# RWKV's state steps: the state is added by an identity product on TensorE, and VectorE only multiplies by the decay

## The chip, the cores and the metric

The kernel runs on one core of one Trainium2 chip. The metric is the device time of one launch in microseconds (us), the median over several runs. A trace of one profiled execution stands beside it. A core has five engines that run their own instruction queues in order and meet at semaphores: TensorE (matrix products; PE in the profile, PEld for its weight loads), VectorE (DVE), ScalarE (ACT), GpSimd (POOL) and SyncE (SP, which here issues transfers).

## The reference, cut to what matters

The program is two transformer-like blocks over 256 tokens of width 1024. The second has an RWKV-7 branch of 8 heads of width 64, whose core is a recurrence over the tokens:

```
def step(S, inp):
    r_t, w_t, k_t, v_t, kk_t, b_t = inp
    sa = jnp.einsum('bhvk,bhk->bhv', S, -kk_t)
    S = S * w_t[:, :, None, :] + sa[..., None] * b_t[:, :, None, :] + v_t[..., None] * k_t[:, :, None, :]
    return S, jnp.einsum('bhvk,bhk->bhv', S, r_t)
```

S is a 64 by 64 matrix for each head. The kernel computes it in four chunks of 64 tokens. Inside a chunk everything is brought into matrix form ahead of time, and only the state goes from chunk to chunk. With keys and values scaled by the decay up to their token, a chunk's end state is (S + btok^T sa + ktok^T vtok) times the decay over the chunk, where sa = xat S + U0.

## The kernel before, in words

The whole program is one `build` function with one hand-ordered instruction list for each engine. There is no planner: what stands ahead in an engine's list is done first, and `wait_ge` on a semaphore holds the engine's whole list. Weights come by SyncE's transfers into a ring of three pages; VectorE and ScalarE split each page into a high and a low part, and TensorE multiplies by them, for most of the span. The small stretch that this change touches is the loop over the four chunks (n = 0 to 3) in the middle of the span, lines 1022 to 1046 on TensorE and 2231 to 2244 on VectorE.

TensorE's list for chunk n: it waits for the state n (`s_sb`); 8 sa products (one for each head, `xat` times `states[n]`, into PSUM banks 2 and 3); it waits until VectorE has added U0 to them and stored sa (`sa_sb`); then 16 state products, for each head `btok` times `sa` and `ktok` times `vtok`, summed in PSUM bank 4 or 5. In chunk 1 the products `y_states(0)` and half of `y_part(0)` (the outputs of the first two chunks) follow, in chunk 2 the other half of `y_part(0)`. Chunk 3 ends after sa, and `y_states(1)` and `y_part(1)` follow.

VectorE's list for chunk n: it waits for the sa products (`sa_mm`) and adds U0 (line 2236); then, for n below 3, it waits for the state products (`ds_mm`), adds `states[n]` to what stands in PSUM into `states[n + 1]` (line 2241), and multiplies that by the decay `wend` in place (line 2242). Ahead of the loop VectorE has `lo_part(2, so, ym_r, ...)`, two instructions of line 1740 that belong to another branch and wait for ScalarE's `ym_hi` (line 1579). Ahead of the loop ScalarE brings U0 from PSUM banks 4 and 5 into SBUF, two instructions of line 1576 that count `u0_sb`. Behind the loop VectorE has four instructions of line 2246, four of 2249 and two of 2256; TensorE's next product (`head_norm`) waits for the last.

All these products are of fp32 numbers. A product of 64 rows deep and 64 wide is a tile of 64*64 in the array, and its place follows from the partitions of its operands (`r0` or `r` for rows) and of its output (`r` or `r0` for columns). In the profile a product is two matmul records and two weight load records. All products are recorded at line 458, the `mm` helper, or at 897 for the transposes.

Of the kernel before, what the change touches and what calls it, by code (L numbers as in the profile page):

```python
# [14 lines left out]
P = 128  # L15
# [11 lines left out]
ALU = mybir.AluOpType  # L27
# [82 lines left out]
def build(nc, t, out):  # L110
    with ExitStack() as ctx:
        S = {n: ctx.enter_context(nc.semaphore(n)) for n in dict.fromkeys(SEMS)}
# [24 lines left out]
        ps = ctx.enter_context(nc.psum_tensor("ps", [P, 8, 512], F32))  # L137

        def at(off, n, base=arena, **kw):
            v = base[:, off:off + n]  # L140
            return v.rearrange(kw.pop("r"), **kw) if kw else v
# [4 lines left out]
        ident = pc[:, 0:128]  # L146
# [12 lines left out]
        def w3(off, a, b=L):  # L159
            return arena[:, off:off + a * b].rearrange("p (a b) -> p a b", a=a)  # L160
# [73 lines left out]
        btok = w3(25120, 2, 512)  # L234
        ktok = w3(26144, 2, 512)
        vtok = w3(27168, 2, 512)
        gram = at(2048, 4096).rearrange("p (n a s) -> p n a s", n=16, a=4)
        mt = at(10752, 1024).rearrange("p (n s) -> p n s", n=16)
        sa = w3(12800, 2, 512)
        yT = w3(13824, 4)  # L240
        states = at(23072, 1280).rearrange("p (n j v) -> p n j v", n=5, j=4)
# [20 lines left out]
        s_sb = at(8192, 4096).rearrange("p (t g n) -> p t g n", t=2, g=16)  # L262
# [39 lines left out]
        wend = small[:, 192:208].rearrange("p (j c) -> p j c", j=4)  # L302
# [140 lines left out]
        def _(pe):  # L443
# [13 lines left out]
            def mm(*args, **kw):  # L457
                mm_last[0] = nc.tensor.matmul(*args, **kw)  # L458
                return mm_last[0]
# [179 lines left out]
            for g in range(3):  # L639
                for q in range(2):  # L640
                    p = ((1, 3), (4, 5), (6, 7))[g][q]
                    pe.wait_ge(loaded[p % RING], 16 * (p // RING + 1))
                    for k in range(4):
                        m = mm(ps[0:2, 4 + g, :], csil[:, 4 * q + k, :], ring[:, p % RING, k // 2, 4 * (k % 2):4 * (k % 2) + 4, :],
                               start=q == 0 and k == 0, stop=q == 1 and k == 3)
                    m.then_inc(S["mod_used"], 1)
                if g == 1:
                    pe.wait_ge(S["pconst_in"], 16)
                    pe.wait_ge(S["start_sb"], START["sum1"])
                    for j in range(4):  # L650
                        for c in range(2):
                            mm(ps[:, 2, 24 + 2 * j + c:25 + 2 * j + c], mcol[c][:, j * P:(j + 1) * P], ones[:, 0:1],
                               start=True, stop=True)
# [30 lines left out]
            for d, kw in enumerate((kw_f, kw_b)):  # L684
                for j in range(4):
                    for tt in range(2):
                        for hh in (2 * j, 2 * j + 1):
                            r = (hh % 2) * 64
                            m = mm(ps[r:r + 64, 2 + d, j * P:(j + 1) * P], kw[:, tt, hh * 64:(hh + 1) * 64],
                                   vc_tok[:, tt, hh * P:(hh + 1) * P], start=tt == 0, stop=tt == 1, skip_group_check=True)  # L690
                m.then_inc(S["state_mm"], 1)
            pe.wait_ge(S["const1_in"], 16)
            for q in range(4):
                mm(ps[:, 4 + q, :], c1("perm"), qraw[:, 2 * q:2 * q + 2, :], start=True,
                   stop=True).then_inc(S["perm_mm"], 1)
# [50 lines left out]
            for n in range(8):  # L746
                b = (2, 3, 4, 5)[n // 2]
                if n % 2 == 0 and b == 5:
                    pe.wait_ge(S["probs"], 8)
                m = mm(ps[:, b, (n % 2) * L:(n % 2 + 1) * L], fT[:, n // 2, (n % 2) * P:(n % 2 + 1) * P], c1("dft_d"),  # L750
                       start=True, stop=True)
# [5 lines left out]
            for gi in range(4):  # L757
                n = 0
                for lt in range(2):
                    for c in range(2):  # L760
                        m = mm(ps[:, 6 + gi // 2, (gi % 2) * L:(gi % 2 + 1) * L],
                               four_a[:, 2 * gi + lt, c * P:(c + 1) * P], dft_l[:, c, lt, :], start=n == 0, stop=n == 3)
# [8 lines left out]
            for q in range(4):  # L771
                pe.wait_ge(S["hn_sq"], q + 1)
                mm(ps[:, (6, 7, 2, 3)[q], :], ones, sq_o[:, 2 * q:2 * q + 2, :], start=True,
                   stop=True).then_inc(S["hn_sqmm"], 1)
# [10 lines left out]
            for k in range(8):  # L785
                if k % 2 == 0:
                    pe.wait_ge(S["xs_sq"], 4 + (k // 2 + 1))
                m = mm(ps[:, 3, 0:L], norm_w[:, k, :], sq[:, k, :], start=k == 0, stop=k == 7)
            m.then_inc(S["xs_mm"], 1)
            for k in range(8):  # L790
                m = mm(ps[:, 2, 0:L], ones, sq[:, k, :], start=k == 0, stop=k == 7)
# [3 lines left out]
            for u in range(6):  # L795
                fm_page(PAGE["rkv"] + u, TURN["rkv"] + u, h)
                if u == 2:
                    pe.wait_ge(S["lora_tanh"], 2)
                    for q in (0, 1, 4, 5):
                        for e in range(2):  # L800
                            m_ = (2 * q + e) % 4
                            half = slice(e * L, (e + 1) * L)
                            if q < 2:
                                m = mm(ps[:, 2 + q, half], wa_up[0:64, m_ * P:(m_ + 1) * P], lora_in[0:64, 0, :], start=True,
                                       stop=True)
                                if e == 1:
                                    m.then_inc(S["lora_mm"], 1)
                                m = mm(ps[:, 4 + q, half], wa_up[64:128, m_ * P:(m_ + 1) * P], zs[64:128, 12, :], start=True,
                                       stop=True)
                            else:  # L810
                                m = mm(ps[:, 2 + q, half], g_up[:, m_ * P:(m_ + 1) * P], lora_in[:, 1, :], start=True,
                                       stop=True)
# [4 lines left out]
            for k in range(8):  # L817
                _, m = three(ps[0:36, T % 2, 0:L], (w_if[0][:, k, :], w_if[1][:, k, :]), (h[0][:, k, :], h[1][:, k, :]),
                             k == 0, k == 7)
# [10 lines left out]
            for tt in range(2):  # L830
                m = nc.tensor.transpose(ps[:, 2, 4 * tt:4 * tt + 4], m_rows[0:4, 4, tt * P:(tt + 1) * P], ident[0:4, 0:4])
            m.then_inc(S["uc_mm"], 1)
            for n in range(4):
                mm(ps[:, 4 + n, :], c2("sel")[0:4, n * P:(n + 1) * P], m_rows[0:4, 5:7, :], start=True,
                   stop=True).then_inc(S["bc_mm"], 1)
# [66 lines left out]
            for m_ in range(8):  # L902
                i, j = m_ // 4, m_ % 4
                for e, par in quarters:
                    r, t0 = blocks[par], i * P + 64 * e
                    m = mm(ps[blocks[e], 6 + par, m_ * 64:(m_ + 1) * 64], ar[r, j, i, 0, blocks[e]],
                           beta[r, j, t0:t0 + 64], start=True, stop=True)
# [30 lines left out]
            for q in range(2):  # L938
                for k in range(8):
                    m = turned(6 + q, k, 8 * q + k)  # L940
# [37 lines left out]
            for i in range(2):  # L978
                for j in range(4):
                    for e, par in quarters:  # L980
                        n = 8 * i + 2 * j + par
                        c = slice((2 * j + par) * 64, (2 * j + par + 1) * 64)
                        m = mm(ps[blocks[par], 2 + 2 * i + e, j * 64:(j + 1) * 64], atok[blocks[e], i, c], XT[blocks[e], n, :],
                               start=True, stop=True)
                m.then_inc(S["xa_mm"], 1)
            for i in range(2):
                for hh in range(8):
                    c = slice(hh * 64, (hh + 1) * 64)
                    for s in blocks:
                        m = mm(ps[s, 6 + i, c], gram[s, 8 * i + hh, 2, :], vtok[s, i, c], start=True, stop=True)  # L990
                m.then_inc(S["xa_mm"], 1)
            pe.wait_ge(S["xa_sb"], 2)
            for i in range(2):
                pe.wait_ge(S["lv_sb"], i + 1)
                for hh in range(8):
                    c = slice(hh * 64, (hh + 1) * 64)
                    for s in blocks:
                        m = mm(ps[s, 4 + i, c], XT[s, 8 * i + hh, :], lv[s, i, c], start=True, stop=True)
# [23 lines left out]
            for n in range(4):  # L1022
                i, r0 = n // 2, (n % 2) * 64
                pe.wait_ge(S["s_sb"], n + 1)
                for hh in range(8):
                    r, j = (hh % 2) * 64, hh // 2
                    c = 256 * (n % 2) + 64 * j
                    m = mm(ps[r0:r0 + 64, 2 + hh % 2, c:c + 64], xat[r:r + 64, j, i, r0:r0 + 64],
                           states[r:r + 64, n, j, :], start=True, stop=True)
                m.then_inc(S["sa_mm"], 1)  # L1030
                pe.wait_ge(S["sa_sb"], n + 1)
                if n == 3:
                    break
                for hh in range(8):
                    r, j, c = (hh % 2) * 64, hh // 2, slice(hh * 64, (hh + 1) * 64)
                    o = ps[r:r + 64, 4 + n % 2, j * 64:(j + 1) * 64]
                    mm(o, btok[r0:r0 + 64, i, c], sa[r0:r0 + 64, i, c], start=True, stop=False)
                    m = mm(o, ktok[r0:r0 + 64, i, c], vtok[r0:r0 + 64, i, c], start=False, stop=True)
                m.then_inc(S["ds_mm"], 1)
                if n == 1:  # L1040
                    turn(TURN["pm"])
                    turn(TURN["pm"] + 1)
                    y_states(0)
                    y_part(0, (0, 1))
                if n == 2:
                    y_part(0, (2, 3)).then_inc(S["y_mm"], 1)
# [25 lines left out]
            for n in range(8):  # L1072
                T = TURN["wq"] + n
                turn(T)
                for s in range(2):
                    m = whole(PAGE["wq"] + n, s, ps[:, T % 2, s * L:(s + 1) * L], ("hraw", 32) if n + s == 0 else None)
# [5 lines left out]
            for n in range(4):  # L1082
                for k in range(4):
                    m = mm(ps[:, 2 + n, k * P:(k + 1) * P], xres[:, 4 * (n % 2) + k, (n // 2) * P:(n // 2 + 1) * P], ident,
                           start=k == 0, stop=False, skip_group_check=True)
# [10 lines left out]
            for tt in range(2):  # L1096
                pe.wait_ge(S["selt_ready"], tt + 1)
                pe.wait_ge(S["placed"], 8)
                for c in range(3):
                    m = nc.tensor.transpose(ps[:, 6 + tt, c * P:(c + 1) * P], selv[:, tt, c, :], ident)  # L1100
# [33 lines left out]
            for q in range(L // 4):  # L1134
                scatter(q)
                n, k = (q - 3) // 14, (q - 3) % 14
# [557 lines left out]
        def _(dve):  # L1694
            V = nc.vector
            TT, STT, TS = V.tensor_tensor, V.scalar_tensor_tensor, V.tensor_scalar
            steps = [0]

            def dv(ins):

                steps[0] += 1
                ins.then_inc(S["dch"], 1)
                dve.wait_ge(S["dch"], steps[0])
# [81 lines left out]
            for q in range(2):  # L1785
                p = 2 * q
# [290 lines left out]
            r = m_rows[0:4]  # L2077
# [153 lines left out]
            for n in range(4):  # L2231
                i, c = n // 2, n % 2
                rr = slice(64 * c, 64 * c + 64)
                dve.wait_ge(S["sa_mm"], n + 1)
                by_row = "p (j e v) -> p e j v"
                TT(sa[rr, i, :].rearrange(by_row, e=2, v=64),  # L2236
                   ps[rr, 2:4, 256 * c:256 * c + 256].rearrange("p e (j v) -> p e j v", v=64),
                   U0[rr, i, :].rearrange(by_row, e=2, v=64), ALU.add).then_inc(S["sa_sb"], 1)
                if n < 3:
                    dve.wait_ge(S["ds_mm"], n + 1)  # L2240
                    dv(TT(states[:, n + 1], states[:, n], ps[:, 4 + c, 0:256].rearrange("p (j v) -> p j v", j=4), ALU.add))
                    TT(states[:, n + 1], states[:, n + 1], wend[:, :, n:n + 1].to_broadcast([P, 4, 64]),
                       ALU.mult).then_inc(S["s_sb"], 1)
                    dve.wait_ge(S["s_sb"], n + 2)
            for m in range(4):
                ins = STT(bon[:, m, :], bon[:, m, :], col("gn_b", m), gT[:, m, :], ALU.add, ALU.mult)
# [405 lines left out]
```

## Time and profile before

| what | value |
|---|---|
| median of three runs | 1713.86 us (1713.19 to 1717.4) |
| the profiled execution's own time | 1715.07 us |
| span in its trace | 1713.2 us |
| mean granted TensorE clock over the span | 0.988 |
| TensorE matmul busy | 1643.1 us, 96% |
| VectorE busy | 1173.3 us, 68% |
| ScalarE busy | 802.0 us, 47% |

Times in the trace run from the start of the span. Busy shares are averages over all stages. The granted clock is a share of the full 2.4 GHz: 1.00 is full, 0.50 is 1.2 GHz. Matmuls are pipelined: a record's duration is its latency, and several records overlap. A tile is written rows*columns of the array, "128*64 128x128" being a tile of 128 rows and 64 columns through which 128 columns of the other operand stream from 128 partitions. "x16" is a count of records.

### The profile page before, as it was taken

To read this page: it belongs to the slowest core of one execution; us is meant where nothing else is said; L and a number is where in the kernel's file an instruction comes from. 1 tells how busy PE (TensorE), PEld (TensorE's weight loads), DVE (VectorE), ACT (ScalarE), POOL (GpSimd) and SP (SyncE) were. 2 spreads that over 40 slices of the span, in tenths; PEclk is the share of its full clock that TensorE was granted. 3 is DMA by queue.
4 is the path that set the end of the run, shared out by engine and by line. 5 is a ranking of instruction groups with operands and counts; after the bars stand their busy time and mean duration, and the time that the engine had idled before them with its cause. 6 is when DMAs were issued, how large, how long until landed. Compare 5 with 4: busy or idle time off the path is not lost.

```text
span 1713.2 us, 32554 instructions
## 1 busy us (share of the span) xinstructions
PE 1643.1 (96%) x12574; PEld 1505.7 (88%) x12574; DVE 1173.3 (68%) x2142; ACT 802.0 (47%) x1221; POOL 99.0 (6%) x124
## 2 busy tenths in 40 slices
PE   7999999999999999979999989999999999999997
PEld 2899978999999999878898877999999999999996
DVE  5646556777756769647498998666666666666665
ACT  2423436566644675324213993444444444444443
POOL 0000000022200001210052000000000000000000
PEclk9999899999999999999999999999999999999999
DMA  8765413545544443203333015555555555555553
GB/s 335 301 240 221 144 53 142 194 172 175 194 173 148 150 146 123 100 4 140 128 127 123 25 50 180 189 193 177 193 186 181 196 178 189 191 178 194 183 184 111
DMA packets 38538, 278.94 MB, mean 163 GB/s; under 512 B 4400, under 2 KB 4528, under 8 KB 5040
## 3 DMA queue, kind: packets, MB, share of 16 engines
q1 hardware_dynamic: 35136, 254.82, 41.5%
q0 software_dynamic: 2304, 16.78, 2.5%
q10 hardware_dynamic: 1008, 6.05, 1.0%
q8 instruction: 68, 1.11, 0.3%
q14 instruction: 22, 0.18, 0.0%
HBM read 276.58 MB, written 1.05 MB: 162 GB/s over the span
## 4 chain that ended last, share of the span: by engine, by line
PE 85%; DVE 8%; ACT 4%; issue 2%; DMA 1%; DVEq 0%; POOL 0%; ACTq 0%; POOLq 0%
PE ps L458 85%; DVE piece L1709 2%; ACT piece L1201 1%; DMA ring<-in_stream 1%; DVE pconst_sb L2453 1%; DVE cols L2453 1%; DVE late L2453 0%; DVE arena L1759 0%; DMA small<-in_cT 0%; ACT arena L1240 0%; DVEq L2453 0%; DVE arena L1795 0%; ACT L1236 0%; DVE arena L1776 0%; DVE arena L1828 0%
## 5 line engine op out<-in xcount | busy, mean ns | idle before, releaser
L458 PEld LDWEIGHTS ps<-h_r,piece 128*128 128x128 f32 x5664 | 699.0, 192 | 22.6 <-issue 10.4
L458 PE MATMUL ps<-h_r,piece 128*128 128x256 f32 x5664 | 708.5, 284 | 7.1 <-DVE piece L1709 4.9
L1709 DVE TENSOR_TENSOR piece<-ring,piece 128x1024 fp32r<-128x1024 f32 x434 | 533.0, 1236 | 255.6 <-ACT piece L1201 254.2
L1201 ACT ACTIVATE piece<-ring 128x1024 fp32r<-128x1024 f32 x432 | 452.5, 1056 | 367.4 <-PE ps L458 361.4
L458 PE MATMUL ps<-piece,late_r 128*128 128x512 f32 x1536 | 370.1, 391 | 1.4 <-DVE late_r L2475 1.4
L458 PEld LDWEIGHTS ps<-piece,late_r 128*128 128x128 f32 x1536 | 281.1, 188 | 55.4 <-issue 1.8
L2470 DVE TENSOR_TENSOR late<-late,arena 128x256 f32<-128x256 f32 x113 | 72.1, 638 | 117.6 <-ACT late L1667 117.6
L1667 ACT ACTIVATE late<-ps 128x256 f32<-128x256 f32 x113 | 43.5, 385 | 200.5 <-PE ps L458 200.5
L458 PE MATMUL ps<-arena,ring 128*128 128x256 f32 x480 | 110.5, 379 | 1.6 <-DVE arena L1776 1.6
L458 PEld LDWEIGHTS ps<-arena,ring 128*128 128x128 f32 x480 | 88.1, 190 | 12.3 <-issue 2.0
L458 PE MATMUL ps<-arena 64*64 64x64 f32 (+5 forms) x904 | 79.3, 292 | 9.6 <-DVE arena L2236 5.6
L458 PEld LDWEIGHTS ps<-arena 64*64 64x64 f32 (+3 forms) x904 | 62.0, 159 | 22.7 <-issue 10.4
L1228 ACT ACTIVATE arena<-ps 128x512 f32<-128x512 f32 x43 | 25.6, 595 | 97.9 <-PE ps L458 97.9
L458 PE MATMUL ps<-ffn_hi,piece 128*128 128x256 f32 x352 | 63.5, 283 | 1.2 <-DVE piece L1709 1.2
L2475 DVE TENSOR_TENSOR late_r<-late,late_r 128x256 fp32r<-128x256 f32 x128 | 54.4, 425 | 4.4
L458 PEld LDWEIGHTS ps<-ffn_hi,piece 128*128 128x128 f32 x352 | 54.9, 192 | 1.4 <-DVE piece L1709 1.4
L458 PE MATMUL ps<-ffn_lo,piece 128*128 128x256 f32 x176 | 49.8, 283 | 0.0
L458 PE MATMUL ps<-mg_hi,piece 128*128 128x256 f32 x256 | 42.8, 284 | 0.5 <-DVE arena L1974 0.5
L458 PEld LDWEIGHTS ps<-piece,h_r 128*128 128x128 f32 x288 | 38.8, 210 | 4.2 <-issue 4.2
L458 PE MATMUL ps<-piece,h_r 128*128 128x256 f32 x288 | 40.1, 302 | 2.2 <-issue 2.2
L2473 DVE CAST late_r<-late 128x256 fp32r<-128x256 f32 x128 | 37.6, 294 | 4.4
L458 PEld LDWEIGHTS ps<-mg_hi,piece 128*128 128x128 f32 x256 | 37.7, 192 | 0.9 <-DVE arena L1974 0.9
(324 smaller groups left out, 1701.9 us busy)
## 6 DMA issues: line engine op xcount, KB each, us to landing
ring<-in_stream SPq DMA_DIRECT2D x240, 1024.0 KB, 4.8
arena<-in_mod POOLq DMA_DIRECT2D x16, 1024.0 KB, 5.5
arena<-in_const ACTq DMA_DIRECT2D x1, 2256.0 KB, 10.2
arena<-in_const ACTq DMA_DIRECT2D x1, 1648.0 KB, 8.9
xres<-in_xT SPq DMA_DIRECT2D x1, 1024.0 KB, 12.1
arena<-in_xT SPq DMA_DIRECT2D x1, 1024.0 KB, 6.9
arena<-in_subk ACTq DMA_DIRECT2D x1, 1024.0 KB, 5.0
out<-arena SPq DMA_DIRECT2D x2, 512.0 KB, 2.7
```

Of the source, the lines that this page charges most:

```text
L458: mm_last[0] = nc.tensor.matmul(*args, **kw)
L1201: A(piece[:, 0, c % 3], ring[:, p % RING, s], ACT.Copy).then_inc(S["hi_ready"], 1)
L1228: A(dst, ps[:, T % 2, src], func, **kw).then_inc(acc_free[T % 2], 1)
L1667: A(gelu_t[:, e % 2, :], ps[:, T % 2, 0:L], ACT.Gelu).then_inc(acc_free[T % 2], 1)
L1709: TT(piece[:, 1, c % 3], ring[:, p % RING, s], piece[:, 0, c % 3].bitcast(F32), ALU.subtract).then_inc(S["lo_ready"], 1)
L2453: ins = TS(col_hot[b % 4][e], iota, selT[:, 1, bass.ds(16 * i + (2 * b + e), 1)], selT[:, 2, bass.ds(16 * i + (2 * b + e), 1)], ALU.is_equ ...
L2470: TT(a_t, ready, G[:, :, bass.ds(LOOP * i + e, 1)].rearrange("p n a -> p (n a)"), ALU.mult).then_inc(S["a_chain"], 1)
L2473: V.tensor_copy(a_r[:, 0, b, :], a_t).then_inc(S["a_chain"], 1)
L2475: TT(a_r[:, 1, b, :], a_t, a_r[:, 0, b, :].bitcast(F32), ALU.subtract).then_inc(S["a_ready"], 1)
```

## The change

For chunks 0 to 2 TensorE issues, right behind the sa products and ahead of the wait for `sa_sb`, for each head an identity product that writes the state into the PSUM sum (`ident[:, r:r + 64]`, all 128 rows of the array and 64 columns), and then the head's `ktok` times `vtok` product, which stood behind the wait before. Behind the wait only `btok` times `sa` is left. As the block writes PSUM bank 4 early, a wait for `u0_sb` is added in chunk 0. Only the first product in each column half of a bank clears it (`start=hh < 2`); the others add or write. VectorE then reads the whole sum from PSUM and multiplies by the decay in one instruction.

```
                 m.then_inc(S["sa_mm"], 1)
+                if n == 0:
+                    pe.wait_ge(S["u0_sb"], 2)
+                if n < 3:
+                    for hh in range(8):
+                        r, j, c = (hh % 2) * 64, hh // 2, slice(hh * 64, (hh + 1) * 64)
+                        o = ps[r:r + 64, 4 + n % 2, j * 64:(j + 1) * 64]
+                        mm(o, ident[:, r:r + 64], states[:, n, j, :], start=hh < 2, stop=False, skip_group_check=True)
+                        mm(o, ktok[r0:r0 + 64, i, c], vtok[r0:r0 + 64, i, c], start=False, stop=False, skip_group_check=True)
                 pe.wait_ge(S["sa_sb"], n + 1)
                 if n == 3:
                     break
                 for hh in range(8):
                     r, j, c = (hh % 2) * 64, hh // 2, slice(hh * 64, (hh + 1) * 64)
                     o = ps[r:r + 64, 4 + n % 2, j * 64:(j + 1) * 64]
-                    mm(o, btok[r0:r0 + 64, i, c], sa[r0:r0 + 64, i, c], start=True, stop=False)
-                    m = mm(o, ktok[r0:r0 + 64, i, c], vtok[r0:r0 + 64, i, c], start=False, stop=True)
+                    m = mm(o, btok[r0:r0 + 64, i, c], sa[r0:r0 + 64, i, c], start=False, stop=True, skip_group_check=True)
                 m.then_inc(S["ds_mm"], 1)
...
                     dve.wait_ge(S["ds_mm"], n + 1)
-                    dv(TT(states[:, n + 1], states[:, n], ps[:, 4 + c, 0:256].rearrange("p (j v) -> p j v", j=4), ALU.add))
-                    TT(states[:, n + 1], states[:, n + 1], wend[:, :, n:n + 1].to_broadcast([P, 4, 64]),
-                       ALU.mult).then_inc(S["s_sb"], 1)
+                    TT(states[:, n + 1], ps[:, 4 + c, 0:256].rearrange("p (j v) -> p j v", j=4),
+                       wend[:, :, n:n + 1].to_broadcast([P, 4, 64]), ALU.mult).then_inc(S["s_sb"], 1)
```

## Rows read from the trace of the kernel before

**Rows 1.** The page: TensorE's busy time, and the chain by engine.
```profile
PE 1643.1 (96%) x12574; PEld 1505.7 (88%) x12574; DVE 1173.3 (68%) x2142; ACT 802.0 (47%) x1221; POOL 99.0 (6%) x124
...
PE 85%; DVE 8%; ACT 4%; issue 2%; DMA 1%; DVEq 0%; POOL 0%; ACTq 0%; POOLq 0%
```

**Rows 2.** Chain in order of time, the state loop: start us, us, what.
```profile
752.81 1.22 PE ps L458 x32
...
754.05 0.43 DVE arena L2241
...
754.51 0.43 DVE arena L2242
...
756.22 0.70 DVE arena L2236
...
756.97 4.67 PE ps L458 x109
...
762.10 0.69 DVE arena L2236
...
765.01 0.70 PE ps L458 x16
...
765.81 0.69 DVE arena L2236
...
770.76 8.40 PE ps L458 x33
```

**Rows 3.** Timeline around the loop: start, us, engine, line, idle before and releaser.
```profile
749.72 0.60 ACT L1576 ACTIVATE arena<-ps 128x512 f32<-128x512 f32 x1 [0.34 <-PE ps L458]
...
752.08 0.68 DVE L2236 TENSOR_TENSOR arena<-ps,arena 64x512 f32<-64x512 f32 x1
...
752.81 1.21 PE L458 MATMUL ps<-arena 64*64 64x64 f32 x32 [2.69 <-DVE arena L2236]
...
759.49 0.42 DVE L2242 TENSOR_TENSOR arena<-arena,small 128x256 f32<-128x256 f32 x1
...
766.56 2.08 PE L458 MATMUL ps<-arena 64*64 64x64 f32 x96 [0.87 <-DVE arena L2236]
```

**Rows 4.** Windows: stretch, length, busy by engine, granted clock, DMA share, GB/s.
```profile
752.81:754.03 1.22, 1.21 (x32) 1.05 (x32) 0.00 (x0) 0.00 (x0) 0.00 (x0) 0.93 0.00 0
...
754.99:756.13 1.14, 1.11 (x16) 0.92 (x16) 0.00 (x0) 0.00 (x0) 0.00 (x0) 0.50 0.00 0
...
756.97:761.64 4.67, 4.66 (x112) 4.52 (x112) 0.84 (x2) 0.60 (x1) 0.00 (x0) 0.60 0.01 4
...
762.84:765.71 2.87, 2.34 (x80) 2.07 (x80) 0.84 (x2) 0.00 (x0) 0.00 (x0) 1.00 0.00 0
```

**Rows 5.** TensorE's timeline in three narrow windows where the tile's shape changes.
```profile
157.71 0.52 PE L458 MATMUL ps<-h_r,piece 128*128 128x256 f32 x3
158.16 0.44 PE L458 MATMUL ps<-arena 128*64 128x128 f32 x4
...
705.42 0.49 PE L897 MATMUL ps<-pconst_sb,arena 128*128 128x128 f32 x3
705.85 0.29 PE L458 MATMUL ps<-arena 64*64 64x64 f32 x4
...
706.59 0.41 PE L458 MATMUL ps<-arena 64*64 64x64 f32 x16
706.94 0.44 PE L897 MATMUL ps<-pconst_sb,arena 128*128 128x128 f32 x2
```

**Rows 6.** Groups by shape, 158 to 162 us: count, busy us, mean ns.
```profile
L458 PE MATMUL ps<-arena 128*64 128x128 f32 x64 | 3.7, 274 | 0.0
L458 PEld LDWEIGHTS ps<-arena 128*64 128x64 f32 x64 | 3.5, 137 | 0.1
```

**Rows 7.** TensorE's timeline: first four records (two tiles, two each) of sa groups.
```profile
765.01 0.33 PE L458 MATMUL ps<-arena,hx 64*64 64x64 f32 x4 [0.51 <-DVE arena L2242]
...
754.99 0.48 PE L458 MATMUL ps<-arena,hx 64*64 64x64 f32 x4 [0.97 <-DVE arena L2242]
```

## The prediction

> **What bounds the kernel now.** I read the page first: TensorE is busy 96% of the span and carries 85% of the chain that ended last, VectorE 8% [rows 1]. That is an average over stages, so it says nothing yet of the state loop, which is a small stretch of some 13 us (752.8 to 765.8) in a span of 1713.2. The reader should therefore go next to the chain in order of time around the loop [rows 2]: it alternates strictly between the two engines. In step 0 VectorE's sum of sa (line 2236) ends at 752.77, TensorE's 16 state products (32 matmul records) take 1.22 us, then VectorE's sum (L2241) and multiply (L2242) take 0.96 us from 754.03 to 754.99, then the 8 sa products (16 records) take 1.14 us in step 1 [rows 4] and 0.70 in step 3, then VectorE's sa sum stands between two TensorE pieces: 756.13 to 756.97, 0.84 us. So here latency bounds, not throughput. Two exceptions: in step 1 VectorE has the new state at 759.49 + 0.42 = 759.91 [rows 3], yet the chain stays on TensorE to 761.64 [rows 2], because y_states(0) and half of y_part(0) are queued ahead of sa of step 2. And behind the loop TensorE is done at 766.56 + 2.08 = 768.64 [rows 3], while the next product starts at 770.76 [rows 2], after VectorE's own tail (lines 2246 to 2256) behind the last sa sum; so a shift of that sum passes to the end one for one. The last view is the granted clock [rows 4]: 0.93 in the first state product (it falls just before its end), 0.50 (1.2 GHz) in step 1's sa products, 0.60 on the mean up to 761.64 (so 1.00 for its last 0.9 us), 1.00 (2.4 GHz) from 762.84 on. What TensorE did before the fall: nothing from 750.12 to 752.81 except wait (the idle time before that record, [rows 3]), since VectorE's sa sum was late behind its ym_lo work.
>
> **The change, part by part.** Removed on VectorE, three times: L2241. What is left reads PSUM and the decay, so I cost it like L2241 (0.42 us, PSUM source) or L2242 (0.42, the same decay operand): one instruction instead of two. The start-to-start distance that goes is 754.51 - 754.05 = 0.46 us [rows 2]. In steps 0 and 2 it is on the path; in step 1 it isn't, as TensorE's y products are later.
>
> Moved on TensorE: the 8 key-value products go from behind the wait for sa to ahead of it, so only 8 products with btok stay behind it. 32 records took 1.22, 16 records of the same form 0.70 [rows 2]; without the start-up, which the stream ahead now takes, I use 0.65. Gain behind the wait 0.57 us a step, if what stands ahead is done by then.
>
> Added: 8 identity products a step, 128 rows deep and 64 wide (128*64), woven one for one with the key-value products (64*64). All 16 stand in TensorE's queue ahead of the btok products, so what they take beyond the 0.84 us window delays those, the y products and everything behind. The cost of that block, W, decides the case, and the trace has no such alternation, so I bound it.
>
> Lower end of W: 32 records like the 32 in 1.22 us, 0.93 when start-up is taken off. A 128*64 product is not slower by itself: 64 of them, of twice the columns, are busy 3.7 us [rows 6], 0.058 each, so two run abreast in the two column halves. Upper end: every change between the shapes empties the array. The rows for that are the places where the shape changes [rows 5]. From 128*128 to 128*64 the new kind starts at 158.16, the last of the old ends at 157.71 + 0.52 = 158.23. From 128*128 to 64*64: 705.85 against 705.91. From 64*64 to 128*128: 706.94 against 707.00. Each time the new shape starts only 0.06 to 0.07 us before the old one's last matmul has ended, while within a shape matmuls of 0.22 to 0.27 us follow each other every few hundredths (32 in 1.22). So a change of shape costs most of a matmul's latency, also where only rows or only columns of the tile change: one of these rows changes only the columns; 128*64 to 64*64 changes only the rows. A stretch of one product (two records in a tile) from its first start to its last end is 0.33 us at full clock, 0.48 at half [rows 7]; minus the 0.07 overlap, 0.26 and 0.41 per product. The block holds 16 products and thus 16 changes (the last product is followed by the same shape, so it needs only 0.16): W = 15 x 0.26 + 0.16 = 4.06 us at full clock, 15 x 0.41 + 0.2 = 6.35 at half. I take 4.06: three of three changes behave so, and nothing in the trace shows two shapes abreast.
>
> The Trainium skill, "TensorEngine Tiling (Array Packing)", Key Properties, says that changing the tiling mode, not just the tile, drains TensorE; the three changes in [rows 5] agree, though none is 128*64 against 64*64. By that rule the sum is the one below, without it the fast rival's. The skill's "TensorE: Matmul & The Clock Gate", Part 3, The mechanism, says weight loads overlap matmuls in flight only in other row groups; an identity of all rows would then expose its loads. [Rows 6] speak against it: 64 loads of 128*64 lie within 3.5 us beside the 3.7 of matmuls, 137 ns each.
>
> The added wait for u0_sb is met when ScalarE's second L1576 ends, 749.72 + 0.60 = 750.32 [rows 3], long before sa of step 0 is summed. Behind it are queued only this block and the btok products. Cost nothing; were it later than 752.77 minus W it would add to step 0, and with W = 4.06 it does set the start.
>
> The sum, with full clock:
> Step 0: block 750.35 to 754.41, btok done 755.06 (before 754.03), multiply and handover 0.96 - 0.46 = 0.50, sa products of step 1 start 755.56 (before 754.99): +0.6.
> Step 1: sa products done 756.26; block starts 0.07 earlier, 756.19 to 760.25; btok done 760.90, last one issued 0.2 before. Then 64 y records: 96 take 2.08 [rows 3], two thirds is 1.4. sa of step 2 starts 762.1 (before about 760.9): +1.2. VectorE would be ready at 761.4, so its shorter work buys nothing here.
> Step 2: sa done 762.75, block 762.68 to 766.74, btok done 767.39, sa of step 3 starts 767.89 against 765.01 [rows 2]: +2.9.
> For W above 2.5 us the sum is close to 3W - 9.3, zero at W = 3.1. Part of what the drained block costs is paid back by the clock: the 2.69 us of waiting goes, so the half clock from 753.9 to 760.7 should go too; this is in the sum, worth about 2 us. The 0.46 us before VectorE's sa sum in step 2 (761.64 to 762.10, [rows 2]) contains some 0.4 of issue time and is off the path after, hidden under W.
> Forecast: +2.9. The profiled execution took 1715.07 at a span of 1713.2, so 1716.1 span, 1718.0 device time; the median shown, 1713.86, lies 1.2 below that execution, which gives 1716.7.
>
> **Rivals.**
> Fast: the two shapes don't drain each other, or the queue runs the next head's other column half abreast. W = 0.93 to 1.2, TensorE's block just fills the 0.84 window, each step gains up to 0.57 + 0.46. Step 0 gives -0.98; with the clock kept, step 1 ends -3.8 (the half clock's 2 us with it) and step 2 -4.8; with one stretch of half clock left, -3.4. Middle -4.1: 1709.8. For it: state products interleaved in pairs in one tile already run two abreast (32 in 1.22). Against: [rows 5]. It decides below W = 3.1.
> Slower: the clock. Before the fall at 753.9 TensorE had waited 2.69 us and then worked 1.1 [rows 3, 4]; nothing shows how it takes many short gaps. If it falls in the block, a product costs 0.41 instead of 0.26: 2.3 us a block, plus 0.44 for sa products (1.14 against 0.70) and about 0.4 for btok and as much for y. Held down through steps 1 and 2 that is some 7.8 more, +10.7 or 1724.5; down about half of it, +6.8, 1720.7. It passes the bound below once it is down for over a third of the two steps. For it: emptying the array leaves gaps between matmuls, 16 in a block. Against: the end of the loop, 762.84 to 765.71, has gaps of its own and kept 1.00 [rows 4].
> Partly drained: some changes overlap, W about 3.1, no change, 1713.9. For it: the start of a shape overlaps 0.07 us already. Against: nothing in the rows lies between.
>
> **How the numbers follow.** Within 0.3% means 5.1 us, about what a measurement of this kernel can tell. Forecast 0.60, slower rival 0.19, fast rival 0.14, partly drained 0.07. The forecast and the partial case are within; the fast rival goes beyond -5.1 only if everything works, 0.05 with the rest; the clock rival is beyond +5.1 in most of its range, 0.15, and the forecast's own high end adds 0.04. So faster 0.05, same 0.76, slower 0.19. The forecast's own range is 1715 to 1719; the range reaches down toward the fast rival and up to the half of the clock rival: 1710.5 to 1721.0, leaving out some 0.1 on either side.
>
> **What would show it.** In the changed trace: identity and key-value records alternate about every 0.26 us instead of abreast; blocks of some 4 us ahead of each btok group; VectorE's sa sum of steps 1 and 2 ends some 3 us before the btok products start, where 0.04 us lies between now; one VectorE instruction of 0.42 between state product and sa products; clock 1.00 from 750 to 768. Wrong if a block is under 2 us (fast rival), or the granted clock in 754 to 767 is near 0.5. The loop's last sa sum at about 768.7 instead of 765.81, and everything behind it the same length, would confirm that the shift passes one for one.

## The result, and the profile after

The changed kernel took 1723.74 us (median of 5 runs, 1719.66 to 1724.62) beside 1713.72 of the kernel before (5 runs). The ratio is 1.0042, 95% interval [1.0028, 1.0056]: slower by 7.2 us, 4.8 to 9.6. Measured again at another time, 12 runs beside 25, it was 1.0026 [1.0015, 1.0037], 4.5 us (2.6 to 6.4). The forecast was +2.9, and 1716.7 in a range up to 1721.0. So the direction was right, and the first median lies outside the range. The prediction gave 0.76 to a change within 5.1 us: the first measurement (7.2) lies beyond that, the second within it.

The profiled execution took 1723.74 us at a span of 1721.8, which is 8.6 more than the span before. To see where, measure a piece that noise ahead of it can't touch. I call it the loop length: from the start of ScalarE's second copy of U0 (749.72 before, [rows 3]) to the start of VectorE's last sa sum (765.81, [rows 2]), 16.09 us. The chain after, start, us, what:

```profile
748.24 0.61 ACT arena L1583
748.84 0.04 issue
748.89 5.34 PE ps L458 x48
754.23 0.02 issue
754.25 0.43 DVE arena L2248
754.69 0.04 issue
754.73 18.76 PE ps L458 x236
...
773.59 0.71 DVE arena L2243
```

The reader is to see two things. Where the chain before alternated every microsecond between the engines [rows 2], TensorE now holds it for 18.76 us without a break: VectorE's sums have vanished from it, though they still take their time. And the loop length is 773.59 - 748.24 = 25.35, 9.26 more than before. The rest of the 8.6: the stretch ahead of the loop came 1.48 earlier (748.24 against 749.72), from the last sa sum to the next product it is 5.25 against 4.95, that product's group takes 8.80 against 8.40, and all behind it is 0.1 longer.

TensorE's timeline in blocks 0, 1 and 2 (the identity and key-value products ahead of the wait; "x2" is one product):

```profile
748.89 0.33 PE L458 MATMUL ps<-arena,pconst_sb 128*64 128x64 f32 x2 [0.26 <-ACT arena L1583]
749.15 0.32 PE L458 MATMUL ps<-arena 64*64 64x64 f32 x2
749.40 0.33 PE L458 MATMUL ps<-arena,pconst_sb 128*64 128x64 f32 x2
...
755.78 0.47 PE L458 MATMUL ps<-arena,pconst_sb 128*64 128x64 f32 x2
756.18 0.47 PE L458 MATMUL ps<-arena 64*64 64x64 f32 x2
756.59 0.47 PE L458 MATMUL ps<-arena,pconst_sb 128*64 128x64 f32 x2
...
766.28 0.33 PE L458 MATMUL ps<-arena,pconst_sb 128*64 128x64 f32 x2
766.53 0.33 PE L458 MATMUL ps<-arena 64*64 64x64 f32 x2
...
769.62 0.47 PE L458 MATMUL ps<-arena 64*64 64x64 f32 x2
770.02 0.47 PE L458 MATMUL ps<-arena,pconst_sb 128*64 128x64 f32 x2
```

A product starts every 0.26 us in block 0, every 0.40 in block 1, and block 2 goes from the one pace to the other at 769.6. Its own duration is 0.33 at the one pace and 0.47 at the other ([rows 7] have 0.33 and 0.48). The windows of the same trace say why (length, busy by engine, granted clock, DMA share, GB/s):

```profile
748.89:752.48 3.59, 3.59 (x28) 2.65 (x29) 1.89 (x3) 0.98 (x2) 0.00 (x0) 1.00 0.02 5
...
755.78:762.20 6.42, 6.42 (x38) 4.66 (x38) 0.70 (x1) 0.00 (x0) 0.00 (x0) 0.50 0.00 0
766.14:769.55 3.41, 3.41 (x30) 2.53 (x27) 0.68 (x1) 0.00 (x0) 0.00 (x0) 1.00 0.01 2
769.55:774.33 4.78, 3.91 (x72) 3.42 (x70) 1.14 (x3) 0.00 (x0) 0.00 (x0) 0.50 0.01 3
```

The clock is at 1.2 GHz from 752.48 to 766.14, and again from 769.55 to 783.20, 27.3 us in all. Ahead of both falls TensorE is busy by its records all the time (3.59 of 3.59, 3.41 of 3.41), but with products of two shapes in turn. The kernel before is at 1.2 GHz from 753.86 to 760.69, and again, behind its loop, from 770.93 to 774.34, 10.2 us in all. Counted from the loop's start the first fall comes at nearly the same place in both, 4.2 us after it and 4.1: what differs is how long the clock stays down, and that in this trace the second fall comes inside the loop.

### The profile page after: what moved, and what is told of

The parts are those of the page before. It is cut to its first block, busy times and chain, and to the rows that moved or that the text cites. A ratio compares the mean times of both kernels' runs of the same rounds, so it can differ in the third digit from the quotient of the medians.

```text
span 1721.8 us, 32647 instructions
## 1 busy us (share of the span) xinstructions
PE 1657.5 (96%) x12622; PEld 1518.4 (88%) x12622; DVE 1172.7 (68%) x2139; ACT 802.4 (47%) x1221; POOL 99.1 (6%) x124
## 3 DMA queue, kind: packets, MB, share of 16 engines
q10 hardware_dynamic: 1008, 6.05, 0.9%
## 4 chain that ended last, share of the span: by engine, by line
PE 86%; DVE 7%; ACT 3%; issue 2%; DMA 1%; DVEq 0%; POOL 0%; ACTq 0%; POOLq 0%
PE ps L458 86%; DVE piece L1716 2%; ACT piece L1208 1%; DVE pconst_sb L2459 1%; DVE cols L2459 1%; DVE late L2459 0%; DVE arena L1766 0%; DMA ring<-in_stream 0%; DMA small<-in_cT 0%; ACT arena L1247 0%; DVEq L2459 0%; DVE arena L1802 0%; ACT L1243 0%; DVE arena L1783 0%; DVE arena L1835 0%
## 5 line engine op out<-in xcount | busy, mean ns | idle before, releaser
L458 PEld LDWEIGHTS ps<-h_r,piece 128*128 128x128 f32 x5664 | 699.2, 192 | 22.5 <-issue 10.2
L458 PE MATMUL ps<-arena 64*64 64x64 f32 (+5 forms) x904 | 88.9, 311 | 4.9 <-DVE arena L1947 1.5
L458 PEld LDWEIGHTS ps<-arena 64*64 64x64 f32 (+3 forms) x904 | 68.2, 175 | 19.6 <-issue 10.4
L458 PE MATMUL ps<-arena,pconst_sb 128*128 128x256 f32 (+2 forms) x150 | 43.9, 417 | 1.1 <-DVE arena L2262 0.8
```

## The experiments

Each kernel has 5 to 12 runs, and the ratio is to runs of the kernel before taken beside them (5 to 30). The spread of a kernel's own runs is some 10 us (the kernel before: 1709.6 to 1719.5 in 30 runs), so a median alone says little here. The table gives the ratio with its 95% interval, and from the one profiled run the loop length with the mean granted clock in it.

| kernel | median us | ratio to before | loop us | clock in loop |
|---|---|---|---|---|
| before | 1713.7 to 1716.5 | 1 | 16.09 | 0.79 |
| changed | 1723.7 | 1.0042 [1.0028, 1.0056] | 25.35 | 0.65 |
| changed, again | 1721.1 | 1.0026 [1.0015, 1.0037] | 23.90 | 0.71 |
| pairs | 1714.2 | 0.9990 [0.9979, 1.0002] | 16.06 | 0.79 |
| grouped | 1711.4 | 0.9972 [0.9958, 0.9986] | 14.22 | 0.76 |
| wide identity | 1712.3 | 0.9975 [0.9965, 0.9986] | 14.27 | 0.76 |
| key-value products ahead only | 1712.4 | 0.9991 [0.9981, 1.0001] | 16.11 | 0.58 |
| filler in the wait | 1714.7, 1714.8 | 0.9998 [0.9989, 1.0007], 0.9992 [0.9982, 1.0002] | 15.51, 15.52 | 0.89, 0.89 |
| woven work in the wait | 1715.5 | 1.0000 [0.9990, 1.0010] | 17.47 | 0.69 |
| dense | 1710.3 | 0.9960 [0.9945, 0.9976] | 13.23 | 0.65 |
| dense with filler | 1708.0, 1708.1 | 0.9954 [0.9939, 0.9968], 0.9959 [0.9946, 0.9971] | 10.60, 10.60 | 1.00, 1.00 |

**Grouped order.** The same 16 products, 2 changes of shape in place of 16.

```
-                    for hh in range(8):
...
+                    for kind in range(2):
+                        for hh in range(8):
...
+                            if kind == 0:
+                                mm(o, ident[:, r:r + 64], states[:, n, j, :], start=hh < 2, stop=False, skip_group_check=True)
+                            else:
+                                mm(o, ktok[r0:r0 + 64, i, c], vtok[r0:r0 + 64, i, c], start=False, stop=False, skip_group_check=True)
```

> All 8 identity products first, then all 8 key-value products: the same work as the changed kernel, 2 changes of tile shape a step in place of 16. Loop length below is from the start of ScalarE's second copy of U0 to the start of the last sa sum on VectorE: 16.1 us before, 25.4 changed. Drain theory (every change of shape empties the array, and the emptied block is what let the clock fall): block 1.1 to 1.3 us at full clock, btok products start about 0.2 us later than VectorE's sa sum would allow, 0.8 us gained in steps 0 and 2 and 0.4 in step 1; loop 11.5 to 13.5, time 1709 to 1711. Work theory (it is the added identity work behind the wait, not its order): loop stays near 25, time near 1722. Clock-by-waiting theory (the clock falls only by TensorE's waits): loop 12 to 13.5 here too, so this run doesn't tell it from the first.

Loop 14.22 against 25.35, with the same records; 1.0042 became 0.9972. TensorE's timeline in the grouped kernel's block 0:

```profile
751.28 0.69 PE L458 MATMUL ps<-arena,pconst_sb 128*64 128x64 f32 x16
751.90 0.68 PE L458 MATMUL ps<-arena 64*64 64x64 f32 x16
```

16 records of one shape take 0.69, where in the changed kernel 2 take 0.33: the block is 1.30 us, not 4.1. The work theory is out. One rival goes by the same order and is not named above: in the changed kernel, too, an identity product and the key-value product behind it write the same place in PSUM. The kernel before speaks against it: there `btok` times `sa` and `ktok` times `vtok` of a head write the same place in turn, in one shape, and 32 records take 1.21 us [rows 3]. And in the changed kernel the next head's identity product, which writes another place, starts as late (749.15 to 749.40). The loop is longer than the 11.5 to 13.5 expected, and its clock was at half from 754.35 to 761.18, 3.7 us behind the loop's start. So the part of the expectation that had the emptied block as the one cause of the fall did not hold: with the blocks short, TensorE waits again (1.14 us ahead of the btok products of step 0), and the clock falls as in the kernel before.

**Pairs.** Identity products of two heads, then their two key-value products: 8 changes.

```
+                    for j in range(4):
+                        for kind in range(2):
+                            for hh in range(2 * j, 2 * j + 2):
...
```

> Identity products of two heads, then key-value products of two heads: 8 changes of shape a step in place of 16, the two products of a pair in different column halves. Drain theory: a pair takes about as long as one product did, 0.26 us at full clock, 0.40 at half, so the block is 8 x 0.26 = 2.0 us at full clock, 3.2 at half; by W: loop near 16.1 - 9.3 + 3 x 2.0 but not below the grouped order, about 13.5 at full clock, up to 19 if the clock falls; time 1711 to 1717. Work theory: as the changed kernel, 25 and 1722. Clock-by-waiting theory: clock full through the loop in a block of 2 us, loop 13 to 14.

TensorE's timeline in block 0, and the windows of blocks 0 and 1:

```profile
750.94 0.34 PE L458 MATMUL ps<-arena,pconst_sb 128*64 128x64 f32 x4 [0.26 <-ACT arena L1587]
751.21 0.33 PE L458 MATMUL ps<-arena 64*64 64x64 f32 x4
751.47 0.34 PE L458 MATMUL ps<-arena,pconst_sb 128*64 128x64 f32 x4
```

```profile
750.94:753.12 2.18, 2.18 (x32) 1.57 (x32) 1.68 (x3) 0.98 (x2) 0.00 (x0) 1.00 0.00 0
755.20:758.14 2.94, 2.94 (x34) 2.12 (x32) 0.69 (x1) 0.00 (x0) 0.00 (x0) 0.51 0.00 0
```

A pair costs what one product did, 0.26 us, as two identity products run abreast in the two column halves. Half the changes, half the block (2.18 us). The price goes with the number of changes, and the loop (16.06) is at the level of before, as is the time.

**One identity product of the whole state.** 128*128, 256 columns, then the key-value products.

```
+                    mm(ps[:, 4 + n % 2, 0:256], ident, states[:, n], start=True, stop=False, skip_group_check=True)
...
-                        mm(o, ident[:, r:r + 64], states[:, n, j, :], start=hh < 2, stop=False, skip_group_check=True)
```

> One identity product of the whole state (128*128, 256 columns) in place of eight of 128*64, then the 8 key-value products: 2 changes of shape a step as in the grouped order, 2 identity records in place of 16. Drain theory: what costs is the number of changes, so this equals the grouped order within 0.1 us a step: loop 14.2 at the same clock, 1710 to 1712. Work theory (number of products or records): 0.3 us a step or more shorter than the grouped order.

The loop is 14.27 us against 14.22 at the same mean clock, with an eighth of the identity records. At 2 changes the count of identity records doesn't matter.

**Only the key-value products ahead of the wait.** No identity; VectorE keeps both instructions.

```
...
+                        mm(o, ktok[r0:r0 + 64, i, c], vtok[r0:r0 + 64, i, c], start=hh < 2, stop=False, skip_group_check=True)
                 pe.wait_ge(S["sa_sb"], n + 1)
...
-                    mm(o, btok[r0:r0 + 64, i, c], sa[r0:r0 + 64, i, c], start=True, stop=False)
-                    m = mm(o, ktok[r0:r0 + 64, i, c], vtok[r0:r0 + 64, i, c], start=False, stop=True)
+                    m = mm(o, btok[r0:r0 + 64, i, c], sa[r0:r0 + 64, i, c], start=False, stop=True, skip_group_check=True)
```

> Only the move of the key-value products ahead of the wait for sa; no identity products, VectorE adds the state and multiplies as before. Drain theory: no change of shape, 8 products fit in the 0.84 us that VectorE's sa sum takes: 0.55 us gained in each of three steps, loop 14.4, time 1712; the half clock after step 0's wait comes as before (TensorE still waits over 2 us). Work theory (products ahead of the wait delay the sa sum or btok): loop 16 or more. If the clock doesn't fall because TensorE works 0.5 us more in the wait, a further 2 us: loop 12.5.

The loop took 16.11, not 14.4. Behind the wait for sa now stand 16 records in place of 32, but this execution was at half clock in 13.6 of its loop's 16.1 us, from 748.25 on. That is in the wait of step 0, which was 1.76 us here and not the 2 and more expected:

```profile
748.79 1.12 PE L458 MATMUL ps<-arena 64*64 64x64 f32 x16 [1.76 <-DVE arena L2242]
```

```profile
748.79:749.94 1.15, 1.12 (x16) 0.93 (x16) 0.00 (x0) 0.00 (x0) 0.00 (x0) 0.50 0.00 0
750.89:752.86 1.97, 1.97 (x32) 1.78 (x32) 0.69 (x1) 0.00 (x0) 0.00 (x0) 0.50 0.00 0
752.88:757.28 4.40, 4.40 (x107) 4.40 (x107) 0.85 (x2) 0.60 (x1) 0.00 (x0) 0.50 0.02 4
757.30:765.32 8.02, 6.46 (x149) 5.89 (x149) 4.97 (x12) 0.60 (x1) 0.00 (x0) 0.50 0.01 3
```

The loop is as long as before with twice the time at half clock (13.6 us against 6.8), which fits a shorter chain; no trace of this kernel at full clock shows it. Over 12 runs the ratio is 0.9991, about a third of what the grouped kernel gives, and its interval reaches 1.0001, so a gain is not shown. A miss of my numbers: I had taken the clock as given and priced only the chain.

**Filler in the wait.** The kernel before, with 40 products in step 0's wait whose results are overwritten.

```
+                if n == 0:
+                    pe.wait_ge(S["u0_sb"], 2)
+                    for _ in range(5):
+                        for hh in range(8):
...
+                            mm(ps[r:r + 64, 4, j * 64:(j + 1) * 64], ktok[0:64, 0, c], vtok[0:64, 0, c], start=True, stop=True)
```

> The kernel before, with 40 products whose results are overwritten (64*64, into PSUM bank 4) in TensorE's wait of step 0, some 2.35 us of work in a wait of 2.7; nothing else changed. It measures what the half clock costs in the kernel before. Clock-by-waiting theory: the granted clock stays 1.00 through the loop, loop 16.1 - 2.0 = 14 us, time 1711.7. If the fall has nothing to do with the wait: loop 16.1, time 1713.7. If the filler runs over the end of the wait: up to 0.3 us added.

> The run with 40 products of one shape in TensorE's wait of step 0 once more, beside the woven one. In its first trace the clock fell 3 us later than in the kernel before and for half as long, and the loop took 15.5 us. If work in the wait keeps the clock up, the loop takes 14.0 to 15.5 here again and the mean granted clock over its runs lies above that of the kernel before; if the rest of the loop is what lets it fall, the mean clock is that of before.

Both times the clock held through step 0 and step 1's sa products and fell only at 758, for 3.4 us and so half as long as before; loop 15.5. It is worth 0.6 us, not 2: the half clock now lay on the long y products. So the wait accounts for where the first fall comes, and not for all of it. Behind the loop the clock fell a second time in both (771.6, 772.0), as it does before (770.9). The time is unchanged within the interval.

**Woven work in the wait.** The same, but with 9 products in the order of the changed kernel's block: identity and key-value in turn.

```
+                    for hh in range(5):
...
+                        mm(ps[r:r + 64, 4, j * 64:(j + 1) * 64], ident[:, r:r + 64], states[:, 0, j, :], start=True, stop=True)
+                        if hh < 4:
+                            mm(ps[r:r + 64, 4, j * 64:(j + 1) * 64], ktok[0:64, 0, c], vtok[0:64, 0, c], start=True, stop=True)
```

> The kernel before, with 9 woven products (identity 128*64 and key-value 64*64 in turn, 9 changes of tile shape) whose results are overwritten in TensorE's wait of step 0, 9 x 0.26 = 2.3 us; the rest as before. Beside it the filler run with as long a stretch of one shape. If the emptied block lets the clock fall by itself, it falls here as in the kernel before, within step 0 or at step 1: loop 16, no gain. If any work keeps it up, it stays as in the filler run: loop 14 to 15.5.

The two fillings of the same wait, woven first, then of one shape:

```profile
751.23:753.61 2.38, 2.38 (x19) 1.70 (x18) 1.88 (x3) 0.98 (x2) 0.00 (x0) 1.00 0.04 7
753.67:755.52 1.85, 1.84 (x32) 1.66 (x32) 0.00 (x0) 0.00 (x0) 0.00 (x0) 0.57 0.00 0
756.49:757.61 1.12, 1.11 (x16) 0.92 (x16) 0.00 (x0) 0.00 (x0) 0.00 (x0) 0.50 0.00 0
```

```profile
751.90:755.53 3.63, 3.63 (x113) 3.47 (x112) 1.89 (x3) 0.99 (x2) 0.00 (x0) 1.00 0.02 5
756.51:757.19 0.68, 0.68 (x16) 0.54 (x16) 0.00 (x0) 0.00 (x0) 0.00 (x0) 1.00 0.00 0
```

Both fill the wait by the records. Behind the woven stretch the clock fell at 753.91, 3.3 us after the loop's start; in the kernel before it falls 4.1 us after it, behind 2.69 us of standing still [rows 3, 4]; behind the other it stayed. The woven loop took 17.47 us, where 16 was expected: from 753.91 it was at half clock for 10.2 us, not 6.8, and it fell again at 767.56, inside the loop. The mean clock over the span is 0.987 (woven, 12 runs), 0.9884 (one shape, 12) and 0.987 (before, 22). This bears out that a woven block doesn't keep the clock up. It rests on three traces and on small means; the times of the two don't differ beyond their intervals.

**The changed kernel again.**

> The changed kernel once more, beside the kernel before on the same chip and beside the other runs of this call. Its blocks (16 products, 16 changes of tile shape) took 0.257 us a product at full clock and 0.403 at half in the first trace. Drain-and-clock theory: the same two prices in this trace, whatever the clock does; 3 to 10 us slower than before depending on how much of blocks 1 and 2 falls at half clock; loop length (second U0 copy to last sa sum) 19 to 26. Free-phase theory (the fall had nothing to do with the blocks): as often as not the clock stays full through the blocks, loop 19, 3 us slower.

Loop 23.90. The clock fell at 752.58, in block 0 and 3.7 us behind the loop's start, and came back at 766.24, behind the dense y products; block 2 then ran at full, and no second fall followed:

```profile
766.85 0.33 PE L458 MATMUL ps<-arena,pconst_sb 128*64 128x64 f32 x2
767.11 0.33 PE L458 MATMUL ps<-arena 64*64 64x64 f32 x2
767.37 0.33 PE L458 MATMUL ps<-arena,pconst_sb 128*64 128x64 f32 x2
```

The free-phase theory expected a loop of 19 as often as not; two traces of two have block 1 wholly at half. That speaks against it, but two traces don't exclude it.

**Dense, and dense with filler.** Wide identity; the key-value products of steps 1 and 2 ahead of the wait for the state; the first two chunks' output products behind the sa products of step 3. The second kernel also has 16 overwritten products in step 0's wait.

```
+                if n in (1, 2):
+                    keys_values(n)
                 pe.wait_ge(S["s_sb"], n + 1)
...
+                    mm(ps[:, 4 + n % 2, 0:256], ident, states[:, n], start=False, stop=False, skip_group_check=True)
+                if n == 3:
+                    turn(TURN["pm"])
+                    turn(TURN["pm"] + 1)
+                    y_states(0)
+                    y_part(0, range(4)).then_inc(S["y_mm"], 1)
                 pe.wait_ge(S["sa_sb"], n + 1)
```

> Wide identity; the key-value products of steps 1 and 2 issued before the wait for the state instead of behind sa; y_states(0) and y_part(0) moved behind the sa products of step 3. Drain theory: ahead of btok stand only 2 changes and one product, some 0.75 us against the 1.1 that VectorE's sa sum needs from TensorE's last issue, so no step waits for TensorE: a step takes 0.70 + 0.84 + 0.70 + 0.50 = 2.74 us at full clock, 1.12 + 0.84 + 1.14 + 0.50 = 3.6 at half. Loop 2.4 + 1.2 + 3 x 2.74 - 1.5 = about 10.5 at full clock, 12.5 to 13 at half; 3 to 5.5 us faster than before. Rival (clock): with no long dense stretch left in the loop the clock, once down, stays down through the loop and the output products: loop 13, and 1 to 2 us lost behind it, 1 to 3 us faster than before.

> As the run before, with 16 products whose results are overwritten in TensorE's wait of step 0. If that wait is what starts the fall: clock full through step 0 and later, loop 10.5 to 11.5 and 1 to 2 us faster than the run before. If the sparse steps themselves let it fall: the same as the run before, only later.

> The fastest version once more, in another call: loop 10.6 us where the clock holds (2.75 us a step), 12 to 13.3 where it doesn't; 5 to 9 us faster than the kernel before.

The chain of the kernel with filler alternates again, one step in 755.77 - 753.01 = 2.76 us (2.74 expected):

```profile
753.01 0.70 DVE arena L2255
...
753.76 0.70 PE ps L458 x19
...
754.49 0.44 DVE arena L2260
...
754.97 0.71 PE ps L458 x16
...
755.77 0.69 DVE arena L2255
```

And the windows of the same stretch in dense (first) and dense with filler:

```profile
752.55:761.48 8.93, 8.37 (x111) 6.45 (x112) 2.23 (x5) 0.00 (x0) 0.00 (x0) 0.50 0.01 3
```

```profile
748.57:758.52 9.95, 8.30 (x195) 6.48 (x197) 4.54 (x9) 0.98 (x2) 0.00 (x0) 1.00 0.01 2
```

Without the filler the clock fell at 752.21, behind step 0's wait, and stayed down through the loop, as the rival said (13.23). The time did better than that rival's 1 to 3 us: 6.9 us, 4.1 to 9.4. With it, it stayed at 2.4 GHz from 748 on in both traces, in the loop and in the product group behind it. This version beats both kernels, by 7 to 8 us against before; its ratio twice excludes 1. The 0.9960 of dense and the 0.9954 and 0.9959 with filler don't differ beyond their intervals, so the times don't show the filler's share of the gain. The traces do, and the mean clock over the span goes the same way: 0.9913 in both series with filler (6 runs each), 0.9895 without (8).

## Why the prediction was right in kind and too small

**The price of a change of shape: right.** 0.26 and 0.41 us a product were forecast, 0.257 and 0.40 measured; W, from the block's start to the first btok product, was forecast as 4.06 at full clock and 6.35 at half; in block 0, nearly all at full, it is 4.0 (748.89 to 752.89), in block 1, at half, 6.05 (755.78 to 761.83), since the last key-value product and the first btok product go abreast:

```profile
761.83 3.63 PE L458 MATMUL ps<-arena 64*64 64x64 f32 x77
```

That three changes in [rows 5], none of them the one in question, carried over is the useful part. The rule of the Trainium skill ("TensorEngine Tiling (Array Packing)", Key Properties), that a change of the tiling mode drains TensorE, agrees for 128*64 against 64*64 as well: the block took 4.0, 2.18 and 1.30 us with 16, 8 and 2 changes.

**VectorE's part: right.** One instruction of 0.42 us; it gains nothing while TensorE's block is the later one.

**The sum: its clock term was the failure.** The prediction said "the 2.69 us of waiting goes, so the half clock from 753.9 to 760.7 should go too", and put about 2 us of gain into the sum. It reasoned from the waiting alone and took the block as work that keeps the clock up. It didn't: the clock fell inside block 0 and stayed down for 13.7 us. The prediction had named a granted clock near 0.5 in 754 to 767 as a sign of being wrong; it was 0.53. Without that term the same sum gives +4.9. The second measurement, 4.5, lies there, but the loops of the two traces grew by 9.3 and 7.8, since the blocks themselves ran in part at half. Counted from the loop's start, the sa products of step 1 start at 6.49 (before 5.27): +1.2, forecast +0.6. VectorE's sa sum of step 2 starts at 18.21 (before 12.38): +5.8, forecast +1.2 for the products ahead of it. The last sa sum: 25.35 against 16.09, +9.3, forecast +2.9. Of the 6.4 too little, the block of step 1 makes 6.05 - 4.06 = 2.0, its sa products 0.4 (1.12 against 0.70, [rows 2, 4] for either clock); the rest I don't split: btok and y products at half, and the end of block 2 and what follows it.

**The slower rival** had just this mechanism, with 0.19, and its prices (+6.8 to +10.7 in the loop) hold the measured 9.3 of the profiled run. Its terms (2.3, 0.44, 0.4 and 0.4 us, twice) add up to 7.1 and not to the 7.8 used, which makes the upper end +10.0; 9.3 lies below that too. What was wrong was its chance. The argument against it, that the end of the loop has gaps and kept 1.00, compared a stretch with many overlapping products of one shape to a block with 16 changes of shape.

**What supports the size.** The two traces of the changed kernel have 25.35 us at a mean clock of 0.65 and 23.90 at 0.71, with 17.7 and 13.7 us of them at half. That is 0.36 us lost for each at half, and none at half would leave 25.35 - 0.36 x 17.7 = 19.0, the forecast at full clock. It is a line through two points, but the pace of the blocks gives the same price: 0.403 us a product in place of 0.257 is 0.36 us lost for each at half. Over many runs the mean clock isn't lower than before (0.9874 against 0.9867 over the span), although both traces have more time at half in the loop (17.7 and 13.7 us against 6.8); the rest of the span makes up for it, and why wasn't followed. The lasting loss of 4.5 us therefore needs no more time at half in all: it fits the blocks' own length, part of them at half clock. How it divides between the two isn't shown.

**The other rivals.** Fast fell with the blocks' 0.26 us. Partly drained fell too: nothing overlapped beyond the 0.07 us. The first ratio (7.2 us) and the second (4.5) differ within their intervals, 4.8 to 9.6 and 2.6 to 6.4, and the clock goes with the difference: of the first five runs three had a mean clock of 0.983 or 0.984 and took 1723.7 to 1724.6, the other two had 0.988 and took 1719.7 and 1720.2; the twelve of the second have 0.9874 on the mean and 1721.1 in the median. An identity of 64*64, which needs no change of shape, wasn't tried.

## What to carry to other kernels

Small products of different tile shapes in turn cost most of a matmul's latency at each change; count the changes in an order, not the products, and group by shape. Before moving work into a window ahead of a wait, add up everything in the block against the window: 0.84 us held 8 products of one shape, but not 16 with 16 changes. And price a latency-bound loop at both clocks: at 2.4 GHz the dense loop took 10.6 us, with 9.3 us of it at half 13.2.

## What the runs showed of the hardware that I had not expected

- TensorE can be busy by every record and still lose its clock: 3.59 of 3.59 us busy, in two shapes by turns, with the fall at its end.
- A stretch of unbroken work at half need not bring the clock back. With only the key-value products ahead it was at half from 748.25 to 765.32, with TensorE busy for 7.00 of the 7.02 us from 750.89 to 757.91 in products of one shape. In the kernel before it rose at 760.69, behind 3.7 us of such products, and in both traces of the changed kernel at 766.1 to 766.2, behind the y products. What tells these apart no run here shows.
- Two 128*64 products in different column halves run abreast although they share all rows: four records in 0.34 us, and in the grouped kernel's 16 records of 0.69 us their weight loads are busy for 0.62 of the same 0.69. The Trainium skill ("TensorE: Matmul & The Clock Gate", Part 3, The mechanism) says that weight loads overlap matmuls in flight only where the row group differs; these rows, as [rows 6] before, go against that.
